# Turning the second attention's outputs and the third output product joined in one block of an eight-stage, one-core kernel

## What is computed

```python
qk = jax.nn.silu(causal_depthwise_conv(jnp.concatenate([q_m, k_m], axis=-1), w_conv[l], b_conv[l]))
...
h_m = rms_norm_2(h_m, g_mlstm_head[l].reshape(MLSTM_HEADS, 1, MLSTM_HEAD_DIM))
h_m = merge_heads(h_m) * jax.nn.sigmoid(o_m)
h_a = merge_heads(moba_attention(split_heads(q_a, MOBA_HEADS), split_heads(k_a, MOBA_HEADS),
                                 split_heads(v_a, MOBA_HEADS)))
mix = jnp.concatenate([h_m, h_a], axis=-1) @ w_out[l]
x = x + gate1 * mix
hn2 = rms_norm_2(x, g_norm2[l]) * (1.0 + scale2) + shift2
ffn = hierarchical_moe(hn2, w_router_group[l], b_router_group[l], w_router_expert[l], ...)
x = x + gate2 * ffn
```

## Time and profile before

| | us |
|---|---|
| median of 3 runs | 1832.65 (1831.44 to 1833.43) |
| profiled execution, its own time | 1826.66 |
| span of that execution in the trace | 1824.9 |
| PE busy | 1686.6 (92%) |
| DVE busy / ACT busy | 771.2 (42%) / 503.1 (28%) |

### The profile page before, as it was taken

One profiled execution on the slowest core, in us unless ns is written; L12 is line 12 of the kernel. 1 busy time (PEld: TensorE's weight loads), 2 busy tenths in 40 slices (PEclk: granted clock), 3 DMA queues, 4 the chain that ended last, 5 costly groups with the idle time before them and its releaser, 6 DMA issues. The chain is left out here.

```text
span 1824.9 us, 21240 instructions
## 1 busy us (share of the span) xinstructions
PE 1686.6 (92%) x8216; PEld 1143.9 (63%) x8217; DVE 771.2 (42%) x1319; ACT 503.1 (28%) x820; POOL 186.0 (10%) x244
## 2 busy tenths in 40 slices
PE   6999999999999999999999999989899999998772
PEld 4788887766776878878877778777533333333220
DVE  6344324768776677423344555353411111111114
ACT  4322324545313222312234433343111111110001
POOL 1020000000111221200003000002111111110101
PEclk9999999989999999999999999999999999999996
DMA  9424220025534677222221321107999997999995
GB/s 304 113 70 138 70 93 1 1 93 184 187 114 162 231 276 253 71 97 99 100 73 35 93 88 59 62 1 288 421 419 419 420 391 297 420 418 420 419 420 212
DMA packets 114533, 366.31 MB, mean 201 GB/s; under 512 B 21759, under 2 KB 25003, under 8 KB 89843
## 3 DMA queue, kind: packets, MB, share of 16 engines
q1 hardware_dynamic: 107199, 351.25, 51.3%
q0 software_dynamic: 5760, 9.02, 1.4%
q10 hardware_dynamic: 1460, 4.49, 0.6%
HBM read 359.85 MB, written 16.84 MB: 206 GB/s over the span
## 5 line engine op out<-in xcount | busy, mean ns | idle before, releaser
L2380 PE MATMUL x_gpa<-x_ring,x_Ta 128*64 128x512 f32 x608 | 138.0, 605 | 14.3 <-DMA x_ring<-in_w_expert_gate_dram 10.3
L2380 PE MATMUL x_upa<-x_ring,x_Ta 128*64 128x512 f32 x608 | 136.8, 599 | 14.1 <-DMA x_ring<-in_w_expert_up_dram 14.0
L2380 PEld LDWEIGHTS x_gpa<-x_ring,x_Ta 128*64 128x64 f32 x608 | 46.1, 139 | 103.2 <-issue 101.2
L2380 PEld LDWEIGHTS x_upa<-x_ring,x_Ta 128*64 128x64 f32 x608 | 46.1, 138 | 102.4 <-issue 102.4
L370 DVE TENSOR_TENSOR p_lo<-p_raw,p_hi 128x2048 fp32r<-128x2048 f32 (+1 forms) x20 | 44.8, 2238 | 138.9 <-ACT p_hi L670 138.9
L377 PE MATMUL fr_p<-p_hi,u_high 128*128 128x512 f32 x224 | 89.1, 398 | 0.2 <-DVE p_lo L370 0.2
L378 PE MATMUL fr_p<-p_lo,u_high 128*128 128x512 f32 x224 | 88.0, 393 | 0.0
L379 PE MATMUL fr_p<-p_hi,u_low 128*128 128x512 f32 x224 | 88.0, 393 | 0.0
L2442 ACT ACTIVATE x_siga<-x_gpa 128x512 f32<-128x512 f32 x19 | 11.3, 597 | 253.8 <-PE x_gpa L2380 253.8
L2405 PE MATMUL x_y0a<-x_ring,x_aTa 128*64 128x512 f32 x304 | 72.8, 599 | 5.4 <-ACT x_aTa L2447 4.5
L670 ACT ACTIVATE p_hi<-p_raw 128x2048 fp32r<-128x2048 f32 (+1 forms) x20 | 37.5, 1873 | 127.5 <-DMA p_raw<-in_w_in_dram 127.5
(11 more groups left out here) (828 smaller groups left out, 3939.0 us busy)
## 6 DMA issues: line engine op xcount, KB each, us to landing
x_ring<-in_w_expert_gate_dram SPq DMA_DIRECT2D x64, 1024.0 KB, 25.9
x_ring<-in_w_expert_up_dram SPq DMA_DIRECT2D x64, 1024.0 KB, 27.6
x_ring<-in_w_expert_down_dram SPq DMA_DIRECT2D x64, 1024.0 KB, 26.1
p_raw<-in_w_in_dram SPq DMA_DIRECT2D x18, 1024.0 KB, 5.1
adaw0m<-in_w_ada_dram SPq DMA_DIRECT2D x6, 2048.0 KB, 10.6
adaw1m<-in_w_ada_dram SPq DMA_DIRECT2D x6, 2048.0 KB, 9.3
ada_first<-in_ada_w_dram SPq DMA_DIRECT2D x8, 1024.0 KB, 5.1
w_raw0m<-in_mlp_w_dram SPq DMA_DIRECT2D x8, 1024.0 KB, 7.2
```

What stands on the lines that cost most here:

```text
L2380: mm = nc.tensor.matmul(ps[CAP * f:CAP * f + CAP, :], self.xT[:, k, CAP * f:CAP * f + CAP], w[m + f][k // 4][:, k % 4, :], start=(k == 0), ...
```

## The change

The turning and the product become one block, `turn_project` with the class `TurnProject`. PE turns the 8 chunks into all 8 banks `dp0` to `dp7`, without waiting for one to be emptied, and then multiplies into the same banks. ACT makes the high part of a chunk (`u_high`) straight out of PSUM, DVE its low part (`u_low`) out of PSUM and the high part; `uT3` as such is no longer written. Bank `b` of the first round waits until chunk `b` has been split. The first weights are split in two halves inside `softmax_attention`: ACT after its rounds 3 and 5, DVE after its rounds 4 and 6. SP loads ring slot 0 when all chunks are turned, slots 1 and 2 right behind weights 2, and slots 3 to 5 after the router weights.

```diff
+    def high_half(self, act, j):
+        act.wait_ge(self.landed[0], 16)
+        half = slice(2 * j, 2 * j + 2)
+        self.nc.scalar.activation(self.hi[0][:, half, :], self.raw[0][:, half, :], ACT.Copy).then_inc(self.half_high, 1)
+
+    def low_half(self, dve, j):
+        dve.wait_ge(self.half_high, j + 1)
+        half = slice(2 * j, 2 * j + 2)
+        ins = low(self.nc.vector, self.lo[0][:, half, :], self.raw[0][:, half, :], self.hi[0][:, half, :])
+        if j == 1:
+            ins.then_inc(self.low_ready, 1)
...
                     rounds(heads[n - 2] if n > 1 else None, heads[n - 1] if n else None, heads[n] if n < len(heads) else None)
+                    if split and n in (4, 6):
+                        split.low_half(dve, n // 2 - 2)
...
                     rounds(heads[n - 1] if n else None, heads[n] if n < len(heads) else None)
+                    if split and n in (3, 5):
+                        split.high_half(act, n // 2 - 1)
...
+class TurnProject:
...
+    def sp(self, sp, ring, load_rest):
+        sp.wait_ge(self.turned, KD)
+        ring.load(sp, 0)
+        sp.wait_ge(self.used, 1)
+        load_rows(self.W, sp, self.w, 2, 0)
+        ring.load(sp, 1)
+        ring.load(sp, 2)
+        sp.wait_ge(self.used, 2)
+        load_rows(self.W, sp, self.w, 3, 1)
+        load_rest(sp)
+
+    def act(self, act, scales):
+        W = self.W
+        for k in range(KD):
+            act.wait_ge(self.turned, k + 1)
+            self.nc.scalar.activation(self.high[:, k, :], self.ps[k][:, :], ACT.Copy,
+                                      scale=1.0 if scales[k] is None else scales[k]).then_inc(self.split_high, 1)
+        for i in range(1, self.rounds):
+            act.wait_ge(W.landed[i % 2], 16 * (i // 2) + 16)
+            self.nc.scalar.activation(W.hi[i % 2][:, :, :], W.raw[i % 2][:, :, :], ACT.Copy).then_inc(W.high_ready, 1)
+
+    def dve_splits(self, dve, scales):
+        v, W = self.nc.vector, self.W
+        for k in range(KD):
+            dve.wait_ge(self.split_high, k + 1)
+            if scales[k] is None:
+                ins = low(v, self.low[:, k, :], self.ps[k][:, :], self.high[:, k, :])
+            else:
+                ins = v.scalar_tensor_tensor(out=self.low[:, k, :], in0=self.ps[k][:, :], scalar=scales[k],
+                                             in1=self.high[:, k, :].bitcast(F32), op0=ALU.mult, op1=ALU.subtract)
+            ins.then_inc(self.split, 1)
+        for i in range(1, self.rounds):
+            dve.wait_ge(W.high_ready, i)
+            low(v, W.lo[i % 2][:, :, :], W.raw[i % 2][:, :, :], W.hi[i % 2][:, :, :]).then_inc(W.low_ready, 1)
+
+    def pe(self, pe, rows):
+        W = self.W
+        for k in range(KD):
+            for t in range(NT):
+                mm = self.nc.tensor.transpose(self.ps[k][:, P * t:P * t + P], rows(t, k), self.C.ident[:, :])
+            mm.then_inc(self.turned, 1)
+        for i in range(self.rounds):
+            first, last = i == 0, i == self.rounds - 1
+            pe.wait_ge(W.low_ready, i + 1)
+            pe.wait_ge(self.split, 2 * i + 2)
+            for b in range(2 * NT):
+                t, n = (b // 2, b % 2) if last else (b % NT, b // NT)
+                if first and b >= 2:
+                    pe.wait_ge(self.split, b + 1)
+                for k in (2 * i, 2 * i + 1):
+                    a = (self.high[:, k, P * t:P * t + P], self.low[:, k, P * t:P * t + P])
+                    mm = matmul3(self.nc, self.ps[NT * n + t][:, :], a, W.get(i, 2 * (k % 2) + n, 0, 512), k == 0, k == KD - 1)
+                if last:
+                    mm.then_inc(self.ready, 1)
+            if not last:
+                mm.then_inc(self.used, 1)
...
-            def beside_o3(sp):
+            def load_rest(sp):
                 load_route(sp, A, R)
-                for c in range(6):
+                for c in range(3, 6):
                     ring.load(sp, c)
```

More of the change, by code:

```diff
@@ L1328, in heads, with softmax_attention @@
                 for i in range(units) for k, br in enumerate(self.branches) for h in range(2)]
-def softmax_attention(nc, C, tag, qT, branches, units=4, bias=None, ahead=None):
+def softmax_attention(nc, C, tag, qT, branches, units=4, bias=None, ahead=None, split=None):
     with Scope(nc) as s:
@@ L3391, in pool, with __init__, tile_added, dve_scales @@
             pool.tensor_tensor(dst, dst, self.tmp[b % 2][:, :], ALU.add).then_inc(self.added, 1)
-def project_out(nc, C, hT, w, gate, tag, W, split, ahead, junk, ssq, var, rstd):
+class TurnProject:
+    def __init__(self, s, nc, C, w, gate, W, high, lowT):
+        self.nc, self.C, self.w, self.gate, self.W, self.high, self.low = nc, C, w, gate, W, high, lowT
+        self.ps = [s.bank(f"dp{b}o3") for b in range(2 * NT)]
+        self.rounds = KD // 2
+        self.tmp = [s.sb(f"dt{i}o3", [P, 512]) for i in range(2)]
+        self.turned, self.split_high, self.split, self.used, self.ready, self.scaled, self.added, self.last_added = [
+            s.sem(f"tp_{n}") for n in ("turned", "split_high", "split", "used", "ready", "scaled", "added", "last_added")]
+    def tile_added(self, t):
+        return (self.added, 2 * t + 2) if t < NT - 1 else (self.last_added, 2)
+    def sp(self, sp, ring, load_rest):
[51 more added lines that the diff above has]
+                mm.then_inc(self.used, 1)
+    def dve_scales(self, dve):
+        for b in range(2 * NT):
+            t, n = b // 2, b % 2
+            dve.wait_ge(self.ready, b + 1)
+            if b >= 2:
+                dve.wait_ge(self.added, b - 1)
+            self.nc.vector.tensor_tensor(self.tmp[b % 2][:, :], self.ps[NT * n + t][:, :], self.gate[:, 512 * n:512 * n + 512],
+                                         ALU.mult).then_inc(self.scaled, 1)
+            if t == NT - 1:
+                dve.wait_ge(self.scaled, b + 1)
+                dst = self.C.h[:, t, 512 * n:512 * n + 512]
+                self.nc.vector.tensor_tensor(dst, dst, self.tmp[b % 2][:, :], ALU.add).then_inc(self.last_added, 1)
+    def pool(self, pool):
+        for b in range(2 * NT - 2):
+            t, n = b // 2, b % 2
+            pool.wait_ge(self.scaled, b + 1)
+            dst = self.C.h[:, t, 512 * n:512 * n + 512]
+            pool.tensor_tensor(dst, dst, self.tmp[b % 2][:, :], ALU.add).then_inc(self.added, 1)
@@ L3397, in project_out, with turn_project @@
+def turn_project(nc, C, rows, scales, w, gate, W, lowT, ring, load_rest, junk, ssq, var, rstd):
     with Scope(nc) as s:
         squares, var_ready, rstd_ready = [s.sem(f"st_{n}") for n in ("squares", "var", "rstd")]
-        O = ProjectOut(s, nc, C, hT, w, gate, tag, W, split, s, [s.bank(f"dp{b}{tag}") for b in range(2 * NT)])
+        high = s.sb("u4_high", [P, KD, TOK], F32R)
+        O = TurnProject(s, nc, C, w, gate, W, high, lowT)
         with nc.Block() as block:
@@ L3402, in _ @@
             def _(sp):
-                O.sp(sp)
-                ahead(sp)
+                O.sp(sp, ring, load_rest)
             @block.scalar
             def _(act):
-                O.act(act)
+                O.act(act, scales)
                 for t in range(NT):
@@ L3416, in _ @@
             def _(pe):
-                O.pe(pe)
+                O.pe(pe, rows)
                 pe.wait_ge(O.scaled, 1)
@@ L3422, in _ @@
             def _(dve):
-                O.dve_splits(dve)
+                O.dve_splits(dve, scales)
                 O.dve_scales(dve)
```

54 lines of the change are left out of this document (5 added, 49 removed).

## The result

The changed kernel came out slower. Its median over 20 runs is 1838.93 us (1829.15 to 1843.94), that of the kernel before, run beside it, 1833.14 us (1830.80 to 1838.41); the ratio is 1.0023, interval 1.0012 to 1.0034. In time that is 4.2 us more (2.2 to 6.2) where 3.3 us less was forecast; the two medians lie 5.8 us apart, and the text goes by the ratio, which has an interval. A later set of 11 runs gave 1.0021 (1.0007 to 1.0035). The profiled execution took 1832.42 us with a span of 1830.7 us, 5.8 more than the span before.

A forecast was written before the change was run, and what follows sets the result against it. PE's unbroken chain of work was taken to bound the kernel until about 1525 us, with a fixed tail of transfers after it. -5.77 + 2.30 + 0.13 = -3.34 us on the median 1832.65 gave 1829.3 us, range 1826.0 to 1832.1.

The forecast's parts named there:

- Term 1: Turning block: first product starts earlier, since bank wait, filling products, barrier, uT3 write and first split pair go: -5.77 us.
- the duration assumed for the unseen operation: Turning block, DVE: PSUM times gain minus high part, not in the trace, taken as 0.75 us, at most 1.23.
- Term 2: Attention: weight-split halves cost nothing on ACT, but DVE's two delay the next logits with nothing to absorb them: +2.30 us.
- the bound from above: Attention, DVE's two halves: highest cost taken as 2 x 1.23 = 2.46 us; the lowest was 0.
- The prediction's rival that the halves would be partly hidden: Attention: more slack before PE's weighing makes halves cheaper; with both hidden -5.6 us in sum, 1827.0 us; chance 0.17.
- PE's 0.1 us in the round: Attention rounds: the copy pT1ma ends at 1193.11, PE's weighing needs it at 1193.22, so PE has 0.1 us of slack.
- Term 3: Product's last round: weights 3 queue behind the ring's four transfers, so PE waits +0.13 us.
- the rival of 0.8 to 2.5 us: Last weights late by a loaded queue: PE waits 0.8 to 2.5 us, about 1830.7 us; chance 0.16.
- 5.0 with eleven behind it: Ring's first transfers: first lands after 5.0 us, fifth 12.7 after its issue, so a full queue adds no landing delay.
- The rule of the Trainium skill that the prediction quoted: Weights 3 landing in a full queue: up to 1.8 us later by memory latency, sum -1.5, about 1831.2 us.
- the standstill of the transfers ahead of the tail: Expert stage, 1520 to 1525 us: transfers stop because the ring is full; its absence would show the forecast wrong.
- each microsecond of PE's chain counts: Ahead of 1525 us: a microsecond off PE's unbroken chain comes out of the total; an earlier transfer is worth nothing.

The follow-up runs named there:

- ring last: Changed kernel with the ring's six first transfers issued behind the last weights and the router's: 1834.70 us, ratio 1.0011 to the kernel before.
- halves alone: Kernel before with only the first weights' split moved as halves into the attention, old turning block kept: 1842.30 us, ratio 1.0055.
- one half: Changed kernel with ACT's halves two rounds earlier and DVE's first half one round earlier, DVE's second still behind round 6: 1831.78 us, ratio 1.0005.
- the control: Kernel before, no halves, with nine small PE products added in each of the two late heads: 1836.76 us, ratio 1.0020.
- the filled one: Changed kernel, halves in place, with nine small products put into PE's idleness in each of the two late heads: 1830.40 us, ratio 0.9980.
- the third: Changed kernel with halves in DVE's idleness, the ring's transfers last and weights, high and low parts aligned to 128 bytes: 1827.31 us, ratio 0.9964.

## Why the prediction was wrong

**Term 1 held.** Forecast -5.77, in the trace -5.93 (9.37 to 3.44). The duration assumed for the unseen operation, 0.75, is the one measured, and no bank waits. The three kernels with the halves hidden and the ring last are 0.0036 to 0.0047 faster than the kernel before; no other part of the change takes time out. That is 6.6 to 8.6 us, more than the traces' own -5.9 and +1.3 for the pitch come to. Up to 1.7 us of it can be a gain that the prediction did not count: the old block's wait of 2.73 us was followed by half clock in two of three traces, and the new block has no such wait. The rest is open.

**Term 2 is the step that failed.** The prediction put the halves at "2 x 1.15 = +2.30 us", with 2.46 as the bound from above. The mechanism inside it was right: the halves stood where nothing absorbed them, each delayed the logits by 1.13 us, and a round with a half that met the full clock took 5.39. The bound was wrong, because it counted DVE's time only. I had noted what PE would do, wait, and not asked what the chip grants an engine that waits. By ratios the halves cost 0.0044 (removed from the heads) and 0.0046 (hidden) in the changed kernel, 8.1 to 8.4 us, and 0.0055, 10 us, alone in the kernel before. Take off their own 2.3 and about 6 to 8 us are left.

Five profiled executions had a half ahead of the logits and unfilled idleness behind it (the changed kernel twice, ring last, halves alone, one half), and all five show half clock in or right behind the late heads, 6.8 to 17 us of it. The kernel before and the eight other executions show none there. Filling that idleness took the loss away and the control shows that filling is no gain otherwise. That the half clock in these heads comes from PE's idleness is therefore shown. It doesn't come behind every pause: the five executions have nine pauses of 0.91 us, and six of them were followed by it. What decides between one pause and the next is not shown; PE's busy share of the 3 us is not it (1.88 with, 1.84 without, in one execution).

The Trainium skill has the mechanism (page "TensorE: Matmul & The Clock Gate", section "A second HAM failure mode: psum-queue depth-cycling"): an engine that idles only briefly, but often enough, between groups of products goes back and forth between half and full clock. The trace agrees in kind, with one pause of 0.91 us beside PE's usual gaps of 0.25 us ahead of 1.2 GHz; the page would have been the rule to weigh against the halves, and the prediction did not look at it.

In the two traces of the changed kernel the clock costs 3.1 us and 7.1 us between the first head's end and the first transpose, beyond the halves' own 2.3, so 6 us in the medians is of the size to be expected; the remainder of a few us in single comparisons is within their intervals.

The prediction's rival that the halves would be partly hidden named the right question and took the wrong place: the slack is not PE's 0.1 us in the round but DVE's 2.06 us one round earlier.

**Term 3 was too small.** +0.13 forecast, +1.19 in the trace, inside the rival of 0.8 to 2.5 us. The step that was off is the landing, "5.0 with eleven behind it ... the load adds nothing there": weights 3 took 7.9 us instead of 6.5. With the ring last they take 5.2. The transfers of the changed kernel at that moment:

```profile
1254.00:1255.00 1.00, 1.00 1.11 293
1255.00:1256.00 1.00, 1.00 1.08 144
1256.00:1257.00 1.00, 1.00 0.13 17
```

(time, granted clock, DMA share, GB/s.) The engines are fully busy at 144 GB/s in place of 420, because packets of another kind travel with the tail of the weights: those of the router's weights, most of 16 or 128 bytes, issued right behind and the only others in the queue. They are not what makes the weights late, though. The packets themselves show it. The weights' last eight packets of 4 KB end one by one, about 0.16 us apart, 6.1 to 7.2 us behind the issue; 64 packets of 16 bytes, a sixteenth of the router's, start at 7.22, as the very last ends. The lag is older than the router's weights: their first packets run at 5.4 us, and the ring's last packets of 8 KB already come one by one, the last beginning at 4.3. The reading is that one of the 16 DMA engines works through its share of the queue about 1.2 us behind the rest, and that the transfer has landed only when it is done. Six of the seven traces with the ring ahead of weights 3 show the same, landing in 7.6 to 8.1 us; in the seventh, the filled one, the last packet ends at 6.05 us and the landing takes 6.68, with the router's weights in the same place. With nothing ahead in the queue, the router's weights behind as ever, it takes 5.2. Term 3 thus had the order and the rate of the queue right and took all of its engines to be done together; why one falls behind is open.

The rule of the Trainium skill that the prediction quoted (page "DMA: Bandwidth & Descriptors", section "Latency and other measured facts", more memory latency under high load) would have put the landing up to 1.8 us later than mine, and it was 1.4 later. The number agrees, the mechanism is not what this trace shows: the last packets take 0.16 us each behind a full queue as behind an empty one, and from the last packet to ACT's start it is 0.67 us here and 0.63 with the ring last.

**A term was missing.** The products' pitch went from 0.227 to 0.233 us, +1.3 us. I had costed the products at nothing, since the change leaves their number and shape as they were. Its cause stays open; three candidates are excluded above.

**The sum again:** -5.9 (turning) + 2.3 (halves) + 6 (half clock behind them) + 1.2 (last weights) + 1.3 (pitch) = +4.9 us, against the measured +4.2 (2.2 to 6.2). The 6 was itself taken from differences between ratios, so this agreement is no proof of its own; without it and the halves the sum is -3.4, and the two kernels that differ from the changed one by the halves' place alone measured -3.9 and -4.2. Nothing was gained or lost behind the product: the standstill of the transfers ahead of the tail is still there, so each microsecond of PE's chain counts, as the prediction had it.

## What to carry to other kernels

Before small work goes on an engine that TensorE waits for, look how much idleness it makes on TensorE and whether that engine has idle time elsewhere in the same loop: two operations of 1.2 us cost 8 us at one place and nothing that could be measured one round earlier. Where the idleness can't be avoided, fill it, and no longer than it is, with products into columns that are overwritten anyway (the filling tried here was longer than the pause and still paid). And judge such an edit by medians of many runs, with the granted clock of each stretch read from the trace: half-clock stretches in stages that the edit does not touch put one execution 3.3 us behind another here.

Of the versions tried, the two with halves hidden and ring last that keep the weights' place have the lowest ratios, 0.9953 (0.9934 to 0.9971) and 0.9961 (0.9948 to 0.9974) of the kernel before, though the intervals do not set them apart from the third, at 0.9964. So the idea of the change is good for 0.3 to 0.5% once its two side effects are taken out.

## What the runs showed of the hardware

- The granted clock fell to 1.2 GHz behind six of nine spells in which PE was idle for 0.91 us on top of its usual gaps (1.83 to 2.14 us busy in the 3.00 around the pause, against 2.5 to 3.0 in the heads of the kernel before). It stayed there for 6.8 to 10.2 us. Behind the other three spells, with 1.82 to 2.02 us busy, it stayed at 2.4 GHz, and it did not fall where the spell was filled. Behind the old block's wait of 2.73 us it fell for 3.4 us in two of three traces.
- The same 192 products of 512 columns followed each other every 0.2267 us in the old block and every 0.2333 in the new one, with the transfers beside them or later and in all three placements of the operands that were tried. In the kernel before both values are found too, 0.2267 in one stage and 0.2333 in another.
- Packets of 16 and 128 bytes, mixed with the last of 4 KB, keep the DMA engines fully busy at a third of the rate (1.08 at 144 GB/s, with 420 for packets of 8 KB).
- A transfer with four others ahead of it in the queue landed 1.1 us or more later than its rate says (7.6 to 8.1 us instead of 6.5) in six of seven traces, because one of the 16 DMA engines reached its last packets about 1.2 us behind the others (7.2 us behind the issue, 6.05 in the seventh trace).
